# First block's attentions with plain float32 products in place of high/low triples and dummy products, and an output projection that takes the FoX heads first

## The reference, cut to what matters

```
proj = rms_norm(h) @ w_in            # q_a k_a v_a | q_b k_b v_b | f_b
o_a  = swa_sink_attention(q_a, k_a, v_a)  # 8 query heads, 2 key heads, window 128
o_b  = forgetting_attention(q_b, k_b, v_b, f_b)  # FoX: 8 heads, causal
mix  = concat(o_a, o_b)
h    = h + rms_norm(mix @ w_out)
```

## Time and profile before

| | |
|---|---|
| runs | 2061.88, 2063.59, 2146.77 us |
| median | 2063.59 us |
| span of the profiled execution | 2061.7 us |
| PE busy (matmuls) | 1867.7 us, 91% |
| PE weight loads busy | 1510.2 us, 73% |
| DVE busy | 1090.7 us, 53% |
| ACT busy | 736.5 us, 36% |
| POOL busy | 143.2 us, 7% |
| chain that ended last | PE 83%, DVE 8%, ACT 3%, issue 3%, POOL 2% |

### The profile page before, as it was taken

How to read it: one execution, slowest core, us unless ns; L and a number is a source line. 1 busy time by engine, 2 the same in 40 slices (tenths; PEclk the granted TensorE clock), 3 DMA queues, 4 the chain that set the end, 5 groups by cost and what they waited for, 6 DMA issues and landing times.

```text
span 2061.7 us, 24986 instructions
## 1 busy us (share of the span) xinstructions
PE 1867.7 (91%) x9011; PEld 1510.2 (73%) x9011; DVE 1090.7 (53%) x1780; ACT 736.5 (36%) x1172; POOL 143.2 (7%) x146
## 2 busy tenths in 40 slices
PE   4999999969999999499999999997689999999993
PEld 3888888738888788277778878875567778788772
DVE  6023776264545432653445876563464447866463
ACT  4123665332222222344552322342435542322422
POOL 3000000120101000210000000103000000000002
PEclk9699999989999999699999999999799999999996
DMA  4212000204565522122112222222121112222220
GB/s 166 88 62 82 2 2 1 92 21 159 190 200 192 175 86 98 41 82 103 62 42 82 82 102 103 82 82 82 48 94 68 59 41 102 92 93 103 82 82 41
DMA packets 29256, 178.56 MB, mean 87 GB/s; under 512 B 3581, under 2 KB 3725, under 8 KB 11742
## 3 DMA queue, kind: packets, MB, share of 16 engines
q1 hardware_dynamic: 20160, 145.76, 20.0%
q0 software_dynamic: 8608, 31.21, 4.8%
q10 hardware_dynamic: 382, 0.19, 0.0%
HBM read 172.33 MB, written 4.78 MB: 86 GB/s over the span
## 4 chain that ended last, share of the span: by engine, by line
PE 83%; DVE 8%; ACT 3%; issue 3%; POOL 2%; ACTq 0%; DVEq 0%; POOLq 0%
PE ps L544 26%; PE ps L545 24%; PE ps L546 24%; PE ps L883 2%; PE ps L552 2%; DVE R L1401 2%; PE ps L868 1%; POOL acc L458 1%; DVE h L1361 1%; ACT w_hi L930 1%; DVE w_lo L1361 1%; PE ps L601 1%; DVE tmp L1368 1%; PE ps L874 1%; DVE Xl L1361 1%
## 5 line engine op out<-in xcount | busy, mean ns | idle before, releaser
L544 PE MATMUL ps<-Xh,w_hi 128*128 128x512 f32 x1640 | 660.0, 402 | 66.1 <-DVE Xl L1361 45.0
L545 PE MATMUL ps<-Xl,w_hi 128*128 128x512 f32 x1640 | 647.5, 395 | 0.0
L546 PE MATMUL ps<-Xh,w_lo 128*128 128x512 f32 x1640 | 647.1, 395 | 0.0
L1361 DVE TENSOR_TENSOR w_lo<-w_raw,w_hi 128x2048 fp32r<-128x2048 f32 x135 | 314.9, 2333 | 331.0 <-ACT w_hi L930 328.5
L544 PEld LDWEIGHTS ps<-Xh,w_hi 128*128 128x128 f32 x1640 | 313.7, 191 | 146.1 <-DVE Xl L1361 40.3
L930 ACT ACTIVATE w_hi<-w_raw 128x2048 fp32r<-128x2048 f32 x135 | 258.2, 1912 | 449.8 <-PE ps L546 449.7
L545 PEld LDWEIGHTS ps<-Xl,w_hi 128*128 128x128 f32 x1640 | 314.4, 192 | 68.0 <-issue 4.3
L546 PEld LDWEIGHTS ps<-Xh,w_lo 128*128 128x128 f32 x1640 | 313.4, 191 | 67.3
L1368 DVE SCALAR_TENSOR_TENSOR cacc<-ain,vec,cacc 128x512 f32<-128x512 f32 x240 | 161.9, 745 | 0.0
L601 PE MATMUL ps<-acc,ones 128*128 128x512 f32 x32 | 22.7, 798 | 79.0 <-POOL acc L458 66.0
L930 ACT ACTIVATE gt<-ps 128x512 f32<-128x512 f32 x48 | 28.2, 597 | 152.9 <-PE ps L546 152.9
(11 more groups left out here) (293 smaller groups left out, 2601.2 us busy)
## 6 DMA issues: line engine op xcount, KB each, us to landing
w_raw<-in_w SPq DMA_DIRECT2D x135, 1024.0 KB, 4.8
ada_w<-in_w_ada POOLq DMA_DIRECT2D x48, 512.0 KB, 4.6
bias_scratch<-brow POOLq DMA_DIRECT2D x2, 1312.0 KB, 5.9
h<-in_xT SPq DMA_DIRECT2D x4, 512.0 KB, 6.4
out<-h SPq DMA_DIRECT2D x1, 2048.0 KB, 6.4
bias<-bias_scratch POOLq DMA_DIRECT2D x1, 1024.0 KB, 6.6
bias<-bias_scratch POOLq DMA_DIRECT2D x1, 512.0 KB, 4.7
cact<-in_c POOLq DMA_DIRECT2D x1, 512.0 KB, 4.5
```

The costliest lines, as they stand in the source:

```text
L544: nc.tensor.matmul(o_, whi, xhi, start=start, stop=False)
L545: nc.tensor.matmul(o_, whi, xlo, start=False, stop=False)
L546: return nc.tensor.matmul(o_, wlo, xhi, start=False, stop=stop)
L1361: return nc.vector.tensor_tensor(o_, a_, b_, op)
```

## The change

1. The split of queries, keys, values and PT is gone, with all its buffers, semaphores and waits. PT and PTm are plain float32, and PE waits on `pt_done`, ACT's copy.
2. Every score and value product is one plain float32 product.
3. All dummy products of the attentions are gone (those around the norms stay).
4. The two heads of a pair write rows 0 to 63 and 64 to 127 of one bank (two banks in turn by pairs). ACT rounds the pair straight from the bank into Xh and DVE takes the difference straight from it. A pair's first value product waits for the pair before the last to be read (`o_lo`).
5. The rows of the output weights are reordered on the host: FoX first. Xh and Xl tile i is pair i, and each product group k of slot 9's first tile waits for tile k alone.

```diff
-                qh, ql = qb_hi[0:66, hd % 2, b * P:(b + 1) * P], Qb_lo[0:66, hd, b * P:(b + 1) * P]
-                if b == 0:
-                    pe.wait_ge(qk_lo, hd + 1)
...
-                mm3(bank(c, NM, c0=T - NM), qh, ql, *keys(0, NM), True, True)
-                return mm3(bank(c + 1, P * (b + 1)), qh, ql, *keys(NM, NM + P * (b + 1)), True, True)
+                q = Qb[0:66, hd, b * P:(b + 1) * P]
+                nc.tensor.matmul(bank(c, NM, c0=T - NM), q, Kb[0:66, hd, 0:NM], start=True, stop=True)
+                return nc.tensor.matmul(bank(c + 1, P * (b + 1)), q, Kb[0:66, hd, NM:NM + P * (b + 1)],
+                                        start=True, stop=True)
...
             def scores(u):
                 if u >= 3:
-                    pe.wait_ge(pt_lo_done, u - 2)
+                    pe.wait_ge(pt_done, u - 2)
...
+            def out_block(hd, b):
+                e = hd % 2
+                return bank(B_O + hd // 2 % 2, P, DH * e, DH * (e + 1), c0=P * b)
+
             def fox_pv(hd, b):
...
-                mm3(o_, vbm_hi[0:NM, e, :], Vm_lo[0:NM, cols], PTm[0:NM, q], PTm_lo[0:NM, q], True, False)
+                nc.tensor.matmul(o_, Vm[0:NM, cols], PTm[0:NM, q], start=True, stop=False)
                 for k in range(b + 1):
-                    last = mm3(o_, vb_hi[:, e, k, :], V_lo[:, k, cols], PT[:, k, q], PT_lo[:, k, q], False, k == b)
+                    last = nc.tensor.matmul(o_, V[:, k, cols], PT[:, k, q], start=False, stop=k == b)
                 return last
...
             def values(u):
 
                 hd, b = u // NB, u % NB
-                if hd >= 2 and b == 0:
-                    pe.wait_ge(o_read[hd % 2], hd // 2)
-                keep_busy(2, bank(B_O + hd % 2, P, c0=P * b))
-                pe.wait_ge(pt_lo_done, u + 1)
-                (fox_pv(hd, b) if hd < HEADS else swa_pv(hd % 2, b)).then_inc(pv_done, 1)
+                if hd >= 4 and hd % 2 == 0 and b == 0:
+                    pe.wait_ge(o_lo, hd // 2 - 1)
+                pe.wait_ge(pt_done, u + 1)
+                (fox_pv if hd < HEADS else swa_pv)(hd, b).then_inc(pv_done, 1)
...
-            keep_busy(12, bank(B_O, P))
             scores(0)
             scores(1)
-            keep_busy(8, bank(B_O, P))
...
-                pair_slot(g, g % 2, fills, xwait=(lambda k: (o_lo, HEADS)) if g == S_OUT else None)
+                pair_slot(g, g % 2, fills, xwait=(lambda k: (o_lo, k + 1)) if g == S_OUT else None)
...
             def out_hi(i):
 
-                for e in range(2):
-                    sc.wait_ge(o_read[e], i + 1)
-                act_(Xh[:, (4 + i) % 8, :], tmp[:, i % 2, :], ACT.Copy).then_inc(o_hi, 1)
+                sc.wait_ge(pv_done, 2 * NB * (i + 1))
+                act_(Xh[:, i, :], bank(B_O + i % 2), ACT.Copy).then_inc(o_hi, 1)
...
             def out_lo(i):
                 ve.wait_ge(o_hi, i + 1)
-                tt(Xl[:, (4 + i) % 8, :], tmp[:, i % 2, :], Xh[:, (4 + i) % 8, :], ALU.subtract).then_inc(o_lo, 1)
+                tt(Xl[:, i, :], bank(B_O + i % 2), Xh[:, i, :], ALU.subtract).then_inc(o_lo, 1)
...
-    rows = np.concatenate(heads + [r(512, 512)])
+    rows = np.concatenate([r(512, 512)] + heads)
```

More of the change, by code:

```diff
@@ L178, in program @@
         R0 = at[0]
[L181 to L189, removed]
+        Qb = sb("Qb", [P, HEADS, T])
+        Kb = sb("Kb", [P, HEADS, NM + T])
         o_qa = at[0]
[L192 to L196, removed]
+        Qa = sb("Qa", [P, 4, T])
+        Ka = sb("Ka", [P, NM + T])
+        V = sb("V", [P, NB, 640])
+        Vm = sb("Vm", [NM, 640])
         o_b0 = at[0]
@@ L356, in program @@
         t_full = sem("t_full")
[L357 to L362, removed]
         pt_done = sem("pt_done")
@@ L689, in swa_scores @@
                 r = slice(kv * DH, (kv + 1) * DH)
-                qh, ql = qa_hi[r, i, b * P:(b + 1) * P], Qa_lo[r, i, b * P:(b + 1) * P]
-                if kv == 0 and b == 0:
-                    pe.wait_ge(qk_lo, HEADS + i + 1)
+                q = Qa[r, i, b * P:(b + 1) * P]
                 k0 = NM + P * max(b - 1, 0)
                 k1 = NM + P * (b + 1)
-                mm3(bank(c, NM, c0=T - NM), qh, ql, ka_hi[r, 0:NM], Ka_lo[r, 0:NM], True, True)
-                return mm3(bank(c + 1, k1 - k0), qh, ql, ka_hi[r, k0:k1], Ka_lo[r, k0:k1], True, True)
+                nc.tensor.matmul(bank(c, NM, c0=T - NM), q, Ka[r, 0:NM], start=True, stop=True)
+                return nc.tensor.matmul(bank(c + 1, k1 - k0), q, Ka[r, k0:k1], start=True, stop=True)
             def scores(u):
                 if u >= 3:
-                    pe.wait_ge(pt_lo_done, u - 2)
+                    pe.wait_ge(pt_done, u - 2)
                 (fox_scores if u < UNITS // 2 else swa_scores)(u).then_inc(s_full, 1)
@@ L728, in swa_pv @@
                 q = slice(P * b, P * (b + 1))
[L729 to L730 removed]
+                nc.tensor.matmul(o_, Vm[0:NM, cols], PTm[0:NM, q], start=True, stop=False)
                 if b:
[L733 to L735 removed]
+                    nc.tensor.matmul(o_, V[:, b - 1, cols], PT[:, 0, q], start=False, stop=False)
@@ L737, in values @@
+                return nc.tensor.matmul(o_, V[:, b, cols], PT[:, min(b, 1), q], start=False, stop=True)
             def values(u):
                 hd, b = u // NB, u % NB
-                if hd >= 2 and b == 0:
-                    pe.wait_ge(o_read[hd % 2], hd // 2)
-                keep_busy(2, bank(B_O + hd % 2, P, c0=P * b))
-                pe.wait_ge(pt_lo_done, u + 1)
-                (fox_pv(hd, b) if hd < HEADS else swa_pv(hd % 2, b)).then_inc(pv_done, 1)
+                if hd >= 4 and hd % 2 == 0 and b == 0:
+                    pe.wait_ge(o_lo, hd // 2 - 1)
@@ L1125, in _ @@
                 pt_unit(u)
-                hd, b = u // NB + 1, u % NB
-                if hd < HEADS and b < 2:
-                    head_hi(hd, b)
-                if hd >= HEADS and b == 0 and hd % 2 == 0 and (hd - HEADS) // 2 < 4:
-                    window_hi((hd - HEADS) // 2)
-                if b == 1 and u > NB:
-                    out_read(hd - 2)
-                    if hd % 2 == 1:
-                        out_hi((hd - 3) // 2)
-            out_read(2 * HEADS - 1)
+                if u % (2 * NB) == 1 and u > 1:
+                    out_hi(u // (2 * NB) - 1)
             out_hi(7)
```

97 lines of the change are left out of this document (6 added, 91 removed).

## The result

The changed kernel's executions took 2126.87, 2127.13, 2144.49 and 2145.11 us, median 2135.81. Those of before beside them were 2061.88 to 2146.77, median 2063.7. The ratio is 1.0354, with an interval of 1.0293 to 1.0415: slower by 3.5%. The forecast was 2028.6, and the time lies far outside its range. It is what the fourth rival gave, 2136 us, to which 6 chances in 100 had gone. (Ratios leave out executions that were disturbed as a whole, which is why the one of before at 2146.77 doesn't enter.)

The account below looks back on a forecast made before the run. PE's rate through its own instructions was taken as the bound. FoX 12.0, SWA 17.1, start 3.7 and end 2.2 gave 35.0 us off 2061.7, so 2026.7; with 1.9 for the median, 2028.6 us, range 2017 to 2042.

Parts of the forecast that it names:

- the fourth rival: Attentions: PE's clock falls without the dummies, 107 us more, 2136 us; chance 0.06, 0.04 of it slower by over 2%.
- against it: Second block's last heads: clock stays at 1.00 with PE idle 2.5 us of 10; in the attentions PE idles less.
- The row that argued for the rival: Stretch of 54 to 70 us: PE stays at 0.50 through 76 gapless products, 0.21 us each against 0.115.
- The start: Before the first transpose: without splits it comes at 201.8 us, not 205.53, gaining 3.7 us; the 20 dummies give nothing.
- FoX head: First half of the attentions: PE's period falls from 10.30 to 8.8 us a head, 12.0 us over eight.
- hand-overs: PE's loss where the next product uses other array rows: 0.26 us a unit in FoX, 0.45 in SWA.
- SWA head: Second half of the attentions: period falls from 10.34 to 8.2 us a head, 17.1 us over eight.
- the loop of DVE and ACT: SWA softmax: 7.98 us a head against PE's 7.8, so it sets the time; 0.2 added for disturbance.
- The end: Last value product to slot 9: FoX first lets slot 9 start at once, gaining 2.2 us.
- The sum at full clock: Whole execution: the gains of both halves, start and end were forecast to total 35.0 us.
- The third rival: Attentions: PE saves only streaming, plain products stream four times against three; 9.0 us there, 2048.7 us in all; chance 0.03.

Follow-up runs that it names:

- b_start: Kernel before with its 12 and 8 start dummies kept and the two in each unit taken out; median 2122.02 us, ratio 1.0283.
- a_start: Changed kernel with the 12 and 8 start dummies put back and none in the units; median 2071.35 us, ratio 1.0016.
- c2: Changed kernel with 12 start dummies after the first two scores and one dummy in each SWA unit of blocks 1 and 3; ratio 0.9866.
- s1: Changed kernel with the 12 and 8 start dummies and one dummy in each SWA unit; median 2046.64 us, ratio 0.994.
- s2: Changed kernel with the 12 and 8 start dummies and two dummies in each SWA unit; median 2053.7 us, ratio 0.9944.
- c1: Changed kernel with 12 start dummies after the first two scores and one dummy in each SWA unit; median 2043.4 us, ratio 0.9917.
- c3: Changed kernel with the 12 and 8 start dummies and one dummy in each SWA unit of blocks 1 and 3 only; ratio 0.9887.
- a_both2: Changed kernel with the 12 and 8 start dummies and two dummies in each unit; 2068.61 to 2070.38 us, ratio 1.0031.
- experiment 8: Kernel before with the projection taking the FoX tiles first and waiting tile by tile; median 2060.69 us, ratio 0.9981.
- experiment 3: Changed kernel with start dummies and two dummies in each unit, as the kernel before has them; ratio 1.0031.
- b_none: Kernel before, triples and splits kept, with all dummy products of the attentions taken out; median 2124.34 us, ratio 1.0297.
- a_unit2: Changed kernel with two dummies in each unit and none in front; median 2076.3 us, ratio 1.0059.

## Why the prediction was wrong, point by point

**The step that failed** is the weighing of the fourth rival. Its mechanism, its place and its price stood in the prediction; what failed is the argument "against it" and the 0.06. That argument was the second block's last heads, plain products and transposes at a clock of 1.00 though PE idles for 2.5 of 10 us, "here PE idles less". It took the share of idle time in a stretch as what brings the clock down. The runs show two things in its place. The first fall came where PE had nothing to do for 2.21 us, in front of the stretch. And a busy PE neither brings the clock back by itself (116.00 of 116 us at 0.50 here, 112.00 of 112 in b_start) nor is sure to keep it: in a_start at 314.5, in the changed kernel at 342.9 and in c2 at 299.1 us it fell with PE busy for the whole 14, 17 and 23 us before. The argument also took one stretch of other products as proof for this one. The stretches that speak on the question side by side, all with PE over 98% busy; a place is known for profiled executions alone, for the others time and mean clock tell that the clock was lost and not where:

| stream | dummies in the units | clock |
|---|---|---|
| triples, before | 2 | held |
| triples, b_start | none | lost at 207.4 us, in the first units |
| plain, FoX, a_start, s1, s2, c1, c2, c3 | none | held in all six profiles |
| plain, SWA, a_start | none | lost in the profile at 314.5 us |
| plain, SWA, c2 and c3 | 1 in every second | lost in 6 of 13, in c2's profile at 299.1 us |
| plain, SWA, s1 and c1 | 1 | held in both profiles, lost or partly lost somewhere in 5 of 18 |
| plain, both halves, a_both2 | 2 | held in 7 of 7 |

That the FoX stream holds is not safe either. Four of the 45 executions of its six kernels took over 2100 us (2108.57, 2144.6, 2154.05 and 2177.24, at mean clocks of 0.890 to 0.916). Losing the whole SWA half costs 8 x (14.83 - 8.32) = 52 us, and on a_start's estimated 2036 this gives 2088, so its 2144.6 must have lost the clock in the FoX half too. No profile shows such an execution. It is the case that the expectation of s1 calls held by luck.

The row that argued for the rival, 54 to 70 us at 0.50 through 76 products without a gap, was read as "it can stay low" and then not weighed. The changed kernel showed the same for 116 us.

**The start.** "The 20 dummies before it ... give nothing of their own" is the second failure, and the dearer one for its size: they are worth 66 us of the profiled execution (2126.87 to 2061.0). In the changed kernel their place is the 2.21 us of idle time and what lies ahead of it, and a cost estimate for dummies in idle time gives nothing, which was right for what they take and said nothing on what they keep. The term itself, 3.7 us, was too large: the change gains 2.35, and the first transpose came at 200.74, even ahead of the forecast 201.8, by luck alone, because the projections ended 2.4 us sooner in this execution. What was overlooked is the wait of ACT: its table load doesn't follow Qa at once but stands behind the first unit's minimum, 1.29 us later (the row at 198.39 us above).

**FoX head.** Forecast 8.8 us at full clock, measured 9.17. The prices of the instructions stand; the hand-overs were mis-sized, 0.35 us a unit (9.17 less 7.76, by four) where 0.26 was taken from bounds of 0 and 0.45. One unit of a_start shows where they are:

```profile
244.63 0.28 PE L676 MATMUL ps<-ident,Pr 128*16 128x128 f32 x1
244.74 0.38 PE L678 MATMUL ps<-ident,Pr 128*128 128x128 f32 x2
244.96 0.29 PE L647 MATMUL ps<-Kb,Qb 66*128 66x16 f32 x2
245.10 1.10 PE L648 MATMUL ps<-Kb,Qb 66*128 66x512 f32 x2
246.14 0.43 PE L690 MATMUL ps<-PTm,Vm 16*64 16x128 f32 x2
246.50 0.43 PE L692 MATMUL ps<-PT,V 128*64 128x128 f32 x2
246.86 0.28 PE L676 MATMUL ps<-ident,Pr 128*16 128x128 f32 x1
```

Transposes start 0.11 apart (244.63 to 244.74, and two in the 0.22 to 244.96), as forecast. But the meta value product, two instructions of 16 rows, takes 0.36 us to the next start (246.14 to 246.50) and the value product of 128 rows takes 0.36 again, each 0.22 by its instructions; the scores take 1.04 where their columns stream for 0.86. Only the meta scores are cheaper than counted, 0.14 for 0.22. Together 0.38 us more in this unit, at the three places where one kind of product follows another: scores to meta values 0.18, meta values to values 0.14, values to transposes 0.14. The last of them is the return from 64 to 128 columns that the prediction kept for its upper bound. A part may be weight loads that wait for ACT's copy, though the matmuls themselves hardly did; the waits of a_start's FoX half (columns as below):

```profile
PEld ps L690 <- ACT PTm L896: 8.3, 14, 0.8
PE ps L676 <- DVE Pr L1286: 0.8, 2, 0.4
```

**SWA head.** Forecast 8.2, measured 8.32, which is near, but not for the reason given. The forecast had PE's own need at 7.8 us and let the loop of DVE and ACT set the time, with PE waiting for DVE's Pr. In a_start's SWA stretch PE waits for nobody (between 206 and 314 us the one row of PE's waits is the 0.8 us above, at the very start), and the chain that ended last lies on PE in every piece of it (278 to 314 us, shares by line):

```profile
by line: PE ps L664 23.2%; PE ps L663 15.2%; PE ps L699 14.9%; PE ps L702 11.1%; PE ps L703 10.7%; PE ps L676 9.8%; PE ps L678 8.8%; PE ps L692 5.0%; PE ps L690 2.0%
```

The loop is nearly as slow, and the view of waits shows only what its two engines have of each other (line, what it waited for, total us, times, longest):

```profile
ACT Pr L896 <- DVE nmax L1436: 12.6, 15, 1.0
DVE rsum L1282 <- ACT esink L896: 10.9, 15, 0.8
```

But DVE's next minimum also needs PE's scores. It starts 0.03 us after they end (298.98 + 0.68 = 299.66), and DVE would have been free up to 0.2 us sooner:

```profile
298.98 0.68 PE L664 MATMUL ps<-Ka,Qa 64*128 64x256 f32 x2
...
299.69 0.51 DVE L1436 CUSTOM_DVE_ANT_0 ps<-ps,bias,nsink 128x272 f32<-128x272 f32 x1
```

The minimum starts within 0.04 us of the end of the scores in 11 of the 15 units between 283 and 312 us. So PE's hand-overs were mis-sized here too, (8.32 - 6.0) / 4 = 0.58 us a unit where 0.45 was taken, and the two errors, PE too cheap and the loop as the bound with 0.2 on it, met near the same number. It is also why a dummy in an SWA unit costs its full price.

**The end.** Forecast 2.2 us, measured 2.4, by experiment 8 alone and in the changed kernel.

**The sum at full clock** would be 8 x 1.13 + 8 x 2.02 + 2.35 + 2.4 = 30.0 us where 35.0 was forecast, so about 2034 us. No kernel reached it, since none without dummies kept the clock. It is worked out, not measured; a_start's estimated 2036 less the 2.7 us of its start dummies comes to nearly the same.

**The fourth rival's price** was near. At the low clock 16.85 us for 16.1 and 14.83 for 14.3; the stretch was forecast at 243 us and took 235.0, because PE ran at full clock for 20.5 us, from the last FoX head into the SWA ones. The factor of 1.83 was luck in part: it set triples at the low clock against dummies at the full one. Like against like it is 16.85 / 9.17 = 1.84 for FoX and 14.83 / 8.32 = 1.78 for SWA. The forecast's 2136 and the median's 2135.81 agree better than the sizes do: the profiled execution is 9 us under it, and the median is lifted by two of 2144 and 2145.

**The passes.** The third rival, that the plain products' fourth pass eats the gain, was given 0.03 as a sum. Its direction is right: at equal dummies and clock (experiment 3) the plain form is slower than the triples, by 0.9 us a FoX head and 0.4 an SWA head, where the rival's fourth pass had 1.31 and 0.99. How much of it is the pass and how much the hand-overs was not taken apart. All that the change could gain inside the units was in the dummies, and those could not all be left out.

## What to carry to other kernels

Before dummy products are counted as time to be saved, find which granted clock they keep: price them as they stand, then price the whole stretch at the low clock, and take the second unless the trace shows the very same stream holding the clock without them. A stream in which PE is never idle can still run at 1.2 GHz; only the granted clock says so, and busy shares and waits look healthy meanwhile. Where dummies are thinned out, put them at the idle time ahead of the stretch first (in a_start they cost some 2.7 us there and the whole execution took 66 less), then into the part that lacks something, and judge the dose over all executions, for a ratio of those that kept the clock promises too much.

## What the runs showed of the hardware that was not expected

- The clock stays at 0.50 with PE busy for 116.00 of 116 us in the changed kernel and for 112.00 of 112 us in b_start. It also falls from 1.00 with PE busy for the 14 us before (a_start, 314.5 us). The Trainium skill (TensorE: Matmul & The Clock Gate, Part 1, HAM oscillation) gives as the rule that PE must have no long idle gaps. The falls at 199.5 us (changed kernel) and 199.9 us (b_none) do lie in gaps, of 2.21 and 3.2 us; but these runs show that the absence of gaps doesn't by itself bring the clock back, and doesn't always keep it.
- Two 128-column dummies a unit brought the clock back after 24 us (a_unit2). The plain products without them needed 122.9 us and lost it again after 20.5.
- With the same start dummies and none in the units the triples lost the clock in the first units (b_start), and the plain products held it to 314.5 us (a_start). Which property of a stream decides was not tried apart: the widths, the row counts of the weights, the number of instructions and the waits in the first units all differ between the two.
- Executions of one kernel fall apart by whether the clock is lost. The old kernel, whose usual time is 2062 to 2071 us with a mean clock of 0.945 to 0.951, took 2093 to 2096 at 0.932 to 0.935 in six of the 55 executions on record and 2144 to 2147 in four, which had 0.908 where it was recorded; one more of 3777 us had a clock of 1.000 and so another cause.
- Where one kind of small product follows another, PE loses 0.14 to 0.18 us (scores to meta values, meta values to values, values to transposes), with a plain product's instructions 0.11 us apart otherwise, in the one unit of a_start shown.
